# Score products of the mixers: the contraction over 128 partitions is replaced by one over the head's 64

## The chip, the cores and the metric

The program runs on one core of one Trainium2 chip. The metric is the device time of one execution in microseconds (us). The engines of the core are named as the profile names them: PE is TensorE's matmul, PEld its weight load, DVE is VectorE, ACT is ScalarE, POOL is GpSimd, SP is SyncE, which issues most of the transfers (DMA).

## The reference

Two blocks follow each other on 256 tokens of width 1024. The first has two layers; each is a SwiGLU, a token mixer and a second SwiGLU, every one with a modulation in front and a gated residual and layer norm behind. The second block has an attention and pooling mixer, a short convolution mixer and, after each, an expert-choice layer of 16 experts. The change touches the token mixer of the first block alone. It has three kinds of heads, four heads of each, and every one begins with products of queries and keys over a head width of 64:

```
# retention, chunks c of 128 tokens
scores = einsum('bhncd,bhnmd->bhncm', qc, kc) * decay_in
# dilated attention (causal windows)
sc = einsum('bhqd,bhqpjd->bhqpj', q_blk, k_g)       # softmax over the windows
# stick breaking
z = einsum('bhqd,bhsd->bhqs', q_blk, kf)            # log_sigmoid, reverse cumsum, exp
# out
y = concatenate([y_ret, y_dil, y_sb], -1) @ w_out
```

All of it is float32.

## The kernel before

Each engine has its own program, written out by hand, and they meet at semaphores. Weights stream from HBM into 12 slots of a tile `W`, with a second stream into `W_mod` for the modulation rows; SP issues both in a fixed order and waits before each transfer until the engines have freed its slot.

The mixer of a layer, on PE, is one straight list. `project(g, t, bank)` multiplies the tokens by 512 columns of w_in (line 768, 8 matmuls of 512 columns). `heads_turned` (line 781) transposes queries and keys of two heads, a pair, so that the 64 components of head 0 lie on partitions 0 to 63 and those of head 1 on 64 to 127. DVE or ACT copies the keys of the pair as they are into `kT` (a part of the tile that the trace calls `scr`) and the queries into `qm`, which has one slice of 128 partitions for each head: only the head's own 64 partitions are written, the other 64 were set to zero at the start. So a product over all 128 partitions gives the scores of that head alone.

There are six pairs b = 0 to 5 in a layer, in this order: dilated, stick, dilated, stick, retention, retention. For each, `scores(b)` makes the products for both heads into two PSUM banks (4 and 5 for even b, 6 and 7 for odd b): for each head one matmul with 128 moving columns and one with 256, either order. DVE then works on the pair (`maxima`, line 1656; `neg_abs`, line 1686; `decayed`, line 1720), ACT takes exponentials, `second(b)` on PE transposes the weights (line 805) or sums the sticks (lines 810 and 811), and `values(b)` multiplies by the values (lines 831 to 833). PE's order around these is: scores(0), project, scores(1), second(0), project, values(0), scores(2), second(1), project, values(1), scores(3), second(2), project, values(2), two times heads_turned, `row_sum` (line 659, 32 output columns in four column groups of the array), second(3), scores(4), values(3), scores(5), values(4), values(5), project, the transposes of the result (line 672) and the product by w_out (line 747).

`values(3)` waits for DVE's `stick_mask(3)` (lines 1692 and 1693), which stands on DVE behind `sticks(3)` (line 1705) and `decayed(4)` (line 1720). `second(1)` waits for DVE's `keeps(1)` (ends on line 1693).

A float32 matmul of the program is two passes in the trace: two weight loads and two MATMUL records.

Of the kernel before, what the change touches and what calls it, by code (L numbers as in the profile page):

```python
# [22 lines left out]
P = 128  # L23
S = 256
# [10 lines left out]
NH = 4  # L35
# [11 lines left out]
RET, DIL, STB = 0, 1, 2  # L47
# [95 lines left out]
def build(nc, A, out):  # L143
    with ExitStack() as ctx:
# [55 lines left out]
        qm = sb("qm", [P, 12, S])  # L200
        psum = ctx.enter_context(nc.psum_tensor("psum", [P, 8, 512], F32))
# [30 lines left out]
        kT = carve(6144, 6, S)  # L232
# [400 lines left out]
        def _(pe):  # L633
# [121 lines left out]
            def mixer(l):  # L755
# [28 lines left out]

                def scores(b):
                    kind, hb = ATT[b]
                    for hh in range(2):
                        q, k_ = qm[:, NH * kind + 2 * hb + hh, :], kT[:, 2 * kind + hb, :]
                        bk = psum[:, 4 + 2 * (b % 2) + hh, :]
                        if kind == DIL:  # L790
                            pe.matmul(bk[:, 0:P], q[:, 0:P], k_[:, 0:P], start=True, stop=True)
                            ins = pe.matmul(bk[:, P:3 * P], q[:, P:S], k_[:, :], start=True, stop=True)
                        else:
                            pe.matmul(bk[:, 0:S], k_[:, 0:P], q[:, :], start=True, stop=True)
                            ins = pe.matmul(bk[:, S:3 * P], k_[:, P:S], q[:, P:S], start=True, stop=True)
                    ins.then_inc(m_pe.sig(f"A{b}"), 1)

                def second(b):
# [104 lines left out]
            for job in range(FIRST_JOBS):  # L903
                pe.wait_ge(mod_taken, job + 1)
                for h in range(2):
                    ins = pe.matmul(psum[:, 2, 8 * job + h:8 * job + 8:2], first_row[job][:, P * h:P * h + P], ident[:, 0:97:32],
                                    start=True, stop=True)
# [19 lines left out]
            for t in range(TT):  # L927
# [4 lines left out]
                for kc in range(KC):  # L932
                    ins = pe.matmul(psum[:, t, 0:256], ctx_uT[:, kc, P * t:P * t + P], part(W[:, s, :], 0, KC, 256)[:, kc, :],
                                    start=(kc == 0), stop=(kc == KC - 1))
                ins.then_inc(m2_pe.sig(f"c{t}"), 1)
            turned(9)
            for t in range(TT):
                for b in range(3):
                    if t == 0 and b < 2:
                        pe.wait_ge(m2_act.s, m2_act.at(f"c{b}"))  # L940
                    for g in (2 * b, 2 * b + 1)[:1 if b == 2 else 2]:
                        s = in_slot("in", MIXIN_S[g]) if t == 0 else MIXIN_S[g]
                        for kc in range(KC):
                            ins = pe.matmul(psum[:, 3 * t + b, 256 * (g % 2):256 * (g % 2) + 256], uT[:, kc, P * t:P * t + P],  # L944
                                            part(W[:, s, :], 0, KC, 256)[:, kc, :], start=(kc == 0), stop=(kc == KC - 1))
# [3 lines left out]
            for i in range(2):  # L949
                for g in (2 * i, 2 * i + 1):  # L950
                    for t in range(TT):
                        ins = pe.matmul(psum[:, 2 + i, S * (g % 2):S * (g % 2) + S], proj2[:, t, 768 + P * g:768 + P * g + P],
                                        pool_c[:, g, t, :], start=(t == 0), stop=(t == TT - 1))
                ins.then_inc(m2_pe.sig(f"pool{i}"), 1)
            for i in range(2):
                pe.wait_ge(m2_dve.s, m2_dve.at(f"pool{i}"))
                for g in (2 * i, 2 * i + 1):
                    ins = pe.matmul(psum[:, 2 + i, S * (g % 2):S * (g % 2) + S], w_grp[:, g, :], pooledT[:, g, :],
                                    start=True, stop=True)
                ins.then_inc(m2_pe.sig(f"grp{i}"), 1)  # L960
            pe.wait_ge(m2_dve.s, m2_dve.at("rope"))
            for n, src in enumerate((ctx_kv[:, 0, 0:P], ctx_kv[:, 1, 0:P], proj2[:, 0, 512:640], proj2[:, 1, 512:640])):
                ins = pe.transpose(psum[:, 4, P * n:P * n + P], src, ident[:, :])
            ins.then_inc(m2_pe.sig("kT"), 1)
            for j in range(4):
                for t in range(TT):
                    c = S * (j % 2) + P * t
                    ins = pe.transpose(psum[:, 5 + j // 2, c:c + P], proj2[:, t, P * j:P * j + P], ident[:, :])
# [17 lines left out]
            for n in range(16):  # L986
# [5 lines left out]
                for c, v in enumerate((ctx_kv[:, 0, kv:kv + HD], ctx_kv[:, 1, kv:kv + HD],  # L992
                                       proj2[:, 0, 512 + kv:512 + kv + HD], proj2[:, 1, 512 + kv:512 + kv + HD])):
                    ins = pe.matmul(psum[:, t, HD * h:HD * h + HD], probT[:, n % 2, P * c:P * c + P], v,
                                    start=(c == 0), stop=(c == 3))
# [4 lines left out]
            for b in range(2):  # L1000
                for q in range(2):
                    for t in range(TT):
                        c = P * (2 * b + q)
                        ins = pe.transpose(psum[:, 4 + b, S * q + P * t:S * q + P * t + P], proj2[:, t, c:c + P], ident[:, :])
# [89 lines left out]
            for fb in range(KC):  # L1094
                if fb >= 2:
                    pe.wait_ge(cv_dve.s, cv_dve.at(f"f{fb - 2}"))
                for n in range(3):
# [3 lines left out]
                    o = psum[:, 4 + 2 * (fb % 2) + n // 2, S * (n % 2):S * (n % 2) + S]  # L1101
                    for kc in range(KC):
                        ins = pe.matmul(o, part(W[:, s, :], 0, KC, 256)[:, kc, P * (fb % 2):P * (fb % 2) + P], uT[:, kc, :],  # L1103
                                        start=(kc == 0), stop=(kc == KC - 1))
# [923 lines left out]
```

## Time and profile before

| | |
|---|---|
| median of 3 runs | 2522.92 us (2522.48 to 2528.18) |
| profiled execution, its own time | 2525.63 us |
| its span, first to last instruction | 2523.8 us |
| granted TensorE clock, mean | 0.881 |
| PE busy | 2078.4 us, 82% |
| DVE busy | 1118.6 us, 44% |
| ACT busy | 528.9 us, 21% |
| first mixer of the first block, first projection to the end of the w_out product | about 250 to 407 us from the start |
| second one | about 837 to 995 us |

Busy times overlap between engines. A row of the timeline that joins several instructions gives the start of the first, and the time to the end of the last; each MATMUL record is longer than the distance to the next one, since they are pipelined, so the cost of a matmul in a stream is read from the distance between starts.

### The profile page before, as it was taken

What the parts mean: (1) busy time and instruction counts of PE and PEld (TensorE: products, weight loads), DVE (VectorE), ACT (ScalarE), POOL (GpSimd) and SP (SyncE); (2) the same over time, 40 slices, a digit from 0 to 9 for tenths busy, and PEclk for the clock granted to TensorE, in tenths of its full rate; (3) what the DMA queues carried; (4) which work ended last, traced back from release to release, by engine and by line L of the source; (5) the groups of instructions that cost most, each with busy time, mean ns of one, the idle gap of its engine ahead of it and who ended that gap; (6) DMA issues with size and microseconds to landing.
All of it is one profiled execution on the core that took longest, in us unless ns stands there. A gap on an engine that the chain in (4) does not pass through costs nothing.

```text
span 2523.8 us, 33380 instructions
## 1 busy us (share of the span) xinstructions
PE 2078.4 (82%) x12372; PEld 1309.9 (52%) x12372; DVE 1118.6 (44%) x1724; ACT 528.9 (21%) x860; POOL 65.2 (3%) x96
## 2 busy tenths in 40 slices
PE   6998988997999887999877777777769777666664
PEld 4997455997999354999754322222238431111111
DVE  3887667788887676877343200000022320000002
ACT  3333133333333132333241100000010110000000
POOL 1000000000000000001000000000000000000000
PEclk9998999998999898999987977777779888888887
DMA  9986855887687765887602999999993389999996
GB/s 343 328 304 226 292 209 202 307 305 252 232 315 261 258 244 185 298 307 259 234 34 83 402 410 410 409 410 410 410 357 152 133 322 410 409 410 410 410 410 255
DMA packets 289371, 758.03 MB, mean 300 GB/s; under 512 B 17616, under 2 KB 125424, under 8 KB 289184
## 3 DMA queue, kind: packets, MB, share of 16 engines
q1 hardware_dynamic: 282368, 737.34, 77.8%
q0 software_dynamic: 6688, 19.78, 2.4%
q8 instruction: 36, 0.59, 0.1%
q14 instruction: 23, 0.19, 0.0%
q10 hardware_dynamic: 256, 0.13, 0.0%
HBM read 756.01 MB, written 1.18 MB: 300 GB/s over the span
## 4 chain that ended last, share of the span: by engine, by line
PE 54%; DMA 21%; SPq 13%; DVE 6%; issue 3%; ACT 2%; DVEq 1%; ACTq 0%
PE psum L707 20%; DMA W<-in_w_exp_up 16%; SPq L503 12%; PE psum L719 9%; PE psum L747 5%; PE psum L768 4%; PE psum L1103 3%; DMA W_mod<-in_mod_w 3%; PE psum L1042 3%; DMA W<-in_w_exp_down 1%; PE psum L944 1%; PE psum L680 1%; SPq L507 1%; ACT uT L1149 1%; PE psum L1054 1%
## 5 line engine op out<-in xcount | busy, mean ns | idle before, releaser
L707 PE MATMUL psum<-parts 128*128 128x256 f32 x4224 | 526.9, 285 | 16.2 <-DVE parts L1556 9.0
L707 PEld LDWEIGHTS psum<-parts 128*128 128x128 f32 x4224 | 524.3, 194 | 23.8 <-issue 17.6
L1042 PE MATMUL psum<-W,scr 128*32 128x512 f32 x2048 | 323.7, 743 | 136.3 <-DMA W<-in_w_exp_up 122.9
L1432 DVE SCALAR_TENSOR_TENSOR mod_acc<-W_mod,cond,mod_acc 128x1024 f32<-128x1024 f32 x196 | 251.8, 1284 | 51.6 <-issue 28.2
L1939 DVE TENSOR_TENSOR scr<-scr,psum 128x256 f32<-128x256 f32 x32 | 13.5, 421 | 581.3 <-ACT scr L1382 581.3
L719 PE MATMUL psum<-parts 128*128 128x512 f32 x1056 | 257.8, 393 | 0.0
L1042 PEld LDWEIGHTS psum<-W,scr 128*32 128x32 f32 x2048 | 53.8, 118 | 379.8 <-DMA W<-in_w_exp_up 287.5
L1556 DVE TENSOR_TENSOR parts<-W,parts 128x1024 fp32r<-128x1024 f32 x176 | 207.0, 1219 | 56.1 <-ACT parts L1179 56.1
L1067 PE MATMUL psum<-W,scr 128*32 128x256 f32 x2048 | 165.8, 463 | 73.6 <-DMA W<-in_w_exp_down 58.5
L719 PEld LDWEIGHTS psum<-parts 128*128 128x128 f32 x1056 | 192.6, 188 | 45.3 <-DVE parts L1569 8.2
L1079 PE MATMUL psum<-scr 128*128 128x512 f32 x256 | 160.1, 782 | 31.7 <-DVE scr L1952 29.7
L1179 ACT ACTIVATE parts<-W 128x1024 fp32r<-128x1024 f32 x176 | 175.7, 1051 | 46.4 <-issue 46.4
L768 PE MATMUL psum<-W,uT 128*128 128x512 f32 x384 | 176.6, 617 | 3.3 <-DVE uT L1476 3.3
L1067 PEld LDWEIGHTS psum<-W,scr 128*32 128x32 f32 x2048 | 65.4, 129 | 168.3 <-DMA W<-in_w_exp_down 102.9
L1382 ACT ACTIVATE scr<-psum 128x256 f32<-128x256 f32 x32 | 12.3, 384 | 612.1 <-PE psum L1042 612.1
L1952 DVE COPY scr<-psum 32x256 f32<-32x256 f32 x64 | 27.3, 426 | 244.6 <-PE psum L1067 244.2
L1079 PEld LDWEIGHTS psum<-scr 128*128 128x128 f32 x256 | 63.3, 262 | 117.7 <-issue 70.3
L768 PEld LDWEIGHTS psum<-W,uT 128*128 128x128 f32 x384 | 75.0, 199 | 93.5 <-issue 93.4
L1198 ACT ACTIVATE att<-psum 128x256 f32<-128x256 f32 x88 | 33.8, 384 | 378.6 <-PE psum L707 378.6
L1569 DVE TENSOR_TENSOR parts<-W,parts 128x1024 fp32r<-128x1024 f32 x88 | 107.2, 1218 | 10.3 <-ACT parts L1191 10.3
L1191 ACT ACTIVATE parts<-W 128x1024 fp32r<-128x1024 f32 x88 | 92.9, 1056 | 43.7 <-PE psum L719 43.7
L747 PE MATMUL psum<-W,uT 128*128 128x512 f32 x192 | 86.6, 611 | 2.7 <-issue 1.9
(283 smaller groups left out, 1641.1 us busy)
## 6 DMA issues: line engine op xcount, KB each, us to landing
W<-in_w_exp_down SPq DMA_DIRECT2D x128, 1024.0 KB
W<-in_w_exp_gate SPq DMA_DIRECT2D x256, 512.0 KB, 14.8
W<-in_w_exp_up SPq DMA_DIRECT2D x256, 512.0 KB, 15.7
W_mod<-in_mod_w SPq DMA_DIRECT2D x123, 1024.0 KB, 5.2
W<-in_ffn_w_gate SPq DMA_DIRECT2D x44, 1024.0 KB, 9.6
W<-in_ffn_w_up SPq DMA_DIRECT2D x44, 1024.0 KB, 12.0
W<-in_ffn_w_down SPq DMA_DIRECT2D x44, 1024.0 KB, 9.2
W<-in_w_in SPq DMA_DIRECT2D x24, 1024.0 KB, 8.5
```

What stands on the lines that cost most here:

```text
L503: sp.dma_start(W[:, s, D * n:D * n + D], w[layer, ds(e, 1), P * s:P * s + P, :] .rearrange("a p n -> p (a n)")).then_inc(landed[s], 16)
L707: ins = pe.matmul(psum[:, 4 + t % 2, S * g:S * g + S], w[:, t % 2, g, kc, :], u[:, kc, :], start=(n == 0 and kc == 0), stop=(n == 2 and kc ...
L719: ins = pe.matmul(psum[:, 2 * tt + h, :], h_[:, t % 2, P * tt:P * tt + P], w[:, t % 2, 512 * h:512 * h + 512], start=(t == 0 and n == 0), ...
L747: ins = pe.matmul(psum[:, 2 * tt + h, :], src[:, kc, P * tt:P * tt + P], w[:, kc % 2, 512 * h:512 * h + 512], start=(kc == 0), stop=(kc == ...
L768: ins = pe.matmul(psum[:, bank, :], uT[:, kc, P * t:P * t + P], part(W[:, s, :], 0, 4, 512)[:, kc % 4, :], start=(kc == 0), stop=(kc == KC ...
L1042: ins = pe.matmul(psum[32 * q:32 * q + 32, 4, :].rearrange("p (g n) -> p g n", g=2), xe_now[:, kc, :], w[:, :, q, :], start=(kc == 0), sto ...
L1067: ins = pe.matmul(psum[32 * q:32 * q + 32, 6, 0:256], e_hT[:, c % 2, 32 * (c // 2):32 * (c // 2) + 32], part(W[:, s, :], 0, 2, D)[:, c % 2 ...
L1079: ins = pe.matmul(psum[:, 2 * tt + h, :], GT[:, P * tt:P * tt + P], R[:, 512 * h:512 * h + 512], start=first, stop=True, skip_group_check= ...
L1179: ins = act.activation(gu_hi[:, t % 2, g, :, :], part(W[:, b + g, :], 0, KC, STEP)[:, :, P * (t % 2):P * (t % 2) + P], copy)
L1432: ins = dve.scalar_tensor_tensor(acc[:, :], w, col, acc[:, :], mul, add)
L1556: ins = dve.tensor_tensor(gu_lo[:, t % 2, g, :, :], part(W[:, b + g, :], 0, KC, STEP)[:, :, P * (t % 2):P * (t % 2) + P], gu_hi[:, t % 2, ...
L1569: dve.tensor_tensor(d_lo[:, t % 2, :], part(W[:, b + 2, :], 0, 2, D)[:, t % 2, :], d_hi[:, t % 2, :].bitcast(F32), sub).then_inc(lo_d, 1)
```

## The change

`scores(b)` reads only the 64 partitions of the head, of `qm` and of `kT` alike, so the contraction is over 64 rows. The loops are turned round: where one head had both its matmuls before the other head, now the first matmul of head 0 is followed by the first of head 1, and then come the two second ones. Head 0 uses the upper 64 rows of the array, head 1 the lower 64. Shapes of the outputs, banks, signals and waits are the same, and the zeros in `qm` are still written.

```
-                    for hh in range(2):
-                        q, k_ = qm[:, NH * kind + 2 * hb + hh, :], kT[:, 2 * kind + hb, :]
-                        bk = psum[:, 4 + 2 * (b % 2) + hh, :]
-                        if kind == DIL:
-                            pe.matmul(bk[:, 0:P], q[:, 0:P], k_[:, 0:P], start=True, stop=True)
-                            ins = pe.matmul(bk[:, P:3 * P], q[:, P:S], k_[:, :], start=True, stop=True)
-                        else:
-                            pe.matmul(bk[:, 0:S], k_[:, 0:P], q[:, :], start=True, stop=True)
-                            ins = pe.matmul(bk[:, S:3 * P], k_[:, P:S], q[:, P:S], start=True, stop=True)
+                    for half in range(2):
+                        for hh in range(2):
+                            rows_ = slice(64 * hh, 64 * hh + 64)
+                            q, k_ = qm[rows_, NH * kind + 2 * hb + hh, :], kT[rows_, 2 * kind + hb, :]
+                            bk = psum[:, 4 + 2 * (b % 2) + hh, :]
+                            if kind == DIL:
+                                o, w, x = ((bk[:, 0:P], q[:, 0:P], k_[:, 0:P]), (bk[:, P:3 * P], q[:, P:S], k_[:, :]))[half]
+                            else:
+                                o, w, x = ((bk[:, 0:S], k_[:, 0:P], q[:, :]), (bk[:, S:3 * P], k_[:, P:S], q[:, P:S]))[half]
+                            ins = pe.matmul(o, w, x, start=True, stop=True)
                     ins.then_inc(m_pe.sig(f"A{b}"), 1)
```

On PE, scores(2) stands between the last product of values(0) (line 833, now 834) and second(1) (line 810, now 811). Before, the four matmuls of a dilated pair alternate between 128 and 256 columns, one head after the other:

```order
L833 MATMUL psum<-scr 128x64
L791 MATMUL psum<-scr,qm 128x128
L792 MATMUL psum<-scr,qm 128x256
L791 MATMUL psum<-scr,qm 128x128
L792 MATMUL psum<-scr,qm 128x256
L810 MATMUL psum<-scr,k_later 128x384 [waits mixer_dve]
```

In the changed kernel the same place on PE reads as follows; `x2` is one matmul for each head, and the sizes are those of the output.

```order
L834 MATMUL psum<-scr 128x64
L796 MATMUL psum<-scr,qm 128x128 x2
L796 MATMUL psum<-scr,qm 128x256 x2
L811 MATMUL psum<-scr,k_later 128x384 [waits mixer_dve]
L812 MATMUL psum<-scr,k_ones 128x128
```

The second matmul of head 0 and the first of head 1 have changed places; nothing has moved across scores(2).

The second place is scores(4) on PE, of a retention pair, between second(3) (line 811, now 812) and values(3), whose first matmul waits for DVE. Before:

```order
L811 MATMUL psum<-scr,k_ones 128x128
L794 MATMUL psum<-qm,scr 128x256 [waits mixer_dve,mixer_act]
L795 MATMUL psum<-qm,scr 128x128
L794 MATMUL psum<-qm,scr 128x256
L795 MATMUL psum<-qm,scr 128x128
L831 MATMUL psum<-scr,tmp 128x64 [waits mixer_dve]
```

The changed kernel has at the same place on PE:

```order
L812 MATMUL psum<-scr,k_ones 128x128
L796 MATMUL psum<-qm,scr 128x256 [waits mixer_dve,mixer_act]
L796 MATMUL psum<-qm,scr 128x256
L796 MATMUL psum<-qm,scr 128x128 x2
L832 MATMUL psum<-scr,tmp 128x64 [waits mixer_dve]
```

Here too only the order within the group is another; the wait ahead of the group and the one behind it stand where they stood.

## Rows read from the trace of the kernel before

**Rows 1.** The page, busy time of the engines and shares of the chain
```profile
PE 2078.4 (82%) x12372; PEld 1309.9 (52%) x12372; DVE 1118.6 (44%) x1724; ACT 528.9 (21%) x860; POOL 65.2 (3%) x96
PE psum L707 20%; DMA W<-in_w_exp_up 16%; SPq L503 12%; PE psum L719 9%; PE psum L747 5%; PE psum L768 4%; PE psum L1103 3%; DMA W_mod<-in_mod_w 3%; PE psum L1042 3%; DMA W<-in_w_exp_down 1%; PE psum L944 1%; PE psum L680 1%; SPq L507 1%; ACT uT L1149 1%; PE psum L1054 1%
```

**Rows 2.** Groups of PE by line and form, the score products of both layers
```profile
L794 PE MATMUL psum<-qm,scr 128*128 128x256 f32 x32 | 9.8, 387 | 0.0
L795 PE MATMUL psum<-qm,scr 128*128 128x128 f32 x32 | 6.1, 274 | 0.0
L792 PE MATMUL psum<-scr,qm 128*128 128x256 f32 x16 | 4.8, 380 | 0.0
L791 PE MATMUL psum<-scr,qm 128*128 128x128 f32 x16 | 3.2, 281 | 0.0
```

**Rows 3.** Stretches of the first mixer: busy time, clock, DMA share
```profile
core 0: us, PE busy (x) PEld busy (x) DVE busy (x) ACT busy (x) POOL busy (x), PEclk, DMA share, GB/s
319.00:370.00 51.00, 49.00 (x212) 30.01 (x209) 36.05 (x90) 17.67 (x25) 4.05 (x5) 0.97 0.72 258
319.00:322.00 3.00, 3.00 (x10) 1.50 (x8) 2.82 (x5) 1.38 (x2) 0.00 (x0) 0.60 0.77 286
```

**Rows 4.** Timeline of PE, first mixer: start, us, what, [idle before]
```profile
318.69 0.87 PE L805 MATMUL psum<-k_ident,att 128*128 128x128 f32 x6 [3.20 <-DVE att L1668]
...
329.25 0.44 PE L791 MATMUL psum<-scr,qm 128*128 128x128 f32 x2
...
330.61 0.81 PE L810 MATMUL psum<-scr,k_later 128*128 128x384 f32 x2
...
354.05 0.60 PE L794 MATMUL psum<-qm,scr 128*128 128x256 f32 x2
354.49 0.38 PE L795 MATMUL psum<-qm,scr 128*128 128x128 f32 x2
354.71 0.60 PE L794 MATMUL psum<-qm,scr 128*128 128x256 f32 x2
355.14 0.38 PE L795 MATMUL psum<-qm,scr 128*128 128x128 f32 x2
357.39 0.41 PE L831 MATMUL psum<-scr,tmp 128*128 128x64 f32 x2 [1.87 <-DVE tmp L1693]
```

**Rows 5.** Timeline of PE around a group in four column tiles (L659)
```profile
350.67 1.04 PE L781 MATMUL psum<-k_ident,scr 128*128 128x128 f32 x8
351.64 0.64 PE L659 MATMUL psum<-mod_acc,k_ones 128*32 128x256 f32 x8
352.21 0.91 PE L810 MATMUL psum<-scr,k_later 128*128 128x384 f32 x2
352.96 0.38 PE L811 MATMUL psum<-scr,k_ones 128*128 128x128 f32 x2
353.18 0.81 PE L810 MATMUL psum<-scr,k_later 128*128 128x384 f32 x2
353.83 0.38 PE L811 MATMUL psum<-scr,k_ones 128*128 128x128 f32 x2
```

**Rows 6.** Timeline of PEld: loads of column tiles, full loads, few rows
```profile
304.20 0.19 PEld L659 LDWEIGHTS psum<-mod_acc,k_ones 128*32 128x32 f32 x8 [2.22 <-DVE mod_acc L1432]
...
305.73 0.30 PEld L791 LDWEIGHTS psum<-scr,qm 128*128 128x128 f32 x2
...
1374.12 0.29 PEld L1023 LDWEIGHTS psum<-k_ident,W_mod 16*128 16x128 f32 x2 [6.75 <-DVE W_mod L1916]
```

**Rows 7.** Timeline of DVE, ahead of second(1) and of values(3)
```profile
327.41 0.42 DVE L1693 TENSOR_TENSOR scr<-scr,k_strict 128x256 f32<-128x256 f32 x1
...
355.56 0.69 DVE L1720 TENSOR_TENSOR att<-psum,k_decay 128x512 f32<-128x512 f32 x1 [0.36 <-PE psum L795]
```

**Rows 8.** Timeline of PE, two projections of 16 passes each
```profile
319.40 8.73 PE L768 MATMUL psum<-W,uT 128*128 128x512 f32 x16
...
332.35 7.03 PE L768 MATMUL psum<-W,uT 128*128 128x512 f32 x16
```

## The prediction, made before the changed kernel ran

> **What bounds the kernel now.** I read the page first: PE is busy 82% of the span, and the chain of waits is led by the two lines of the SwiGLUs' matmuls (L707 and L719, 29% together), then by the expert weights (DMA and SP's queue for them, 28% in the first two entries) [rows 1]. The lines of the score products do not appear among the chain's first fifteen. Then the groups by form: the score products are 96 records, 48 matmuls of two passes, and their durations add up to 23.9 us [rows 2]. That sum counts overlaps twice, since a record is longer than the distance to the next; the timeline gives the real price. In scores(4) the starts are 354.05, 354.49, 354.71 and 355.14 [rows 4]: two passes of 256 columns take 0.44 us, two of 128 take 0.22, one head 0.65, a group 1.31. Twelve groups are at most 12 x 1.36 = 16.3 us, 0.6% of the time. The stretches come next: from 319 to 370 us PE is busy for 49.00 of 51.00 us at a granted clock of 0.97 [rows 3], so in this part of a mixer PE is the bound, and what PE saves there is saved, as far as nothing else takes over.
>
> **Which groups count.** scores(0) and scores(1) lie ahead of a wait of 3.20 us for DVE's weighting (L1668) [rows 4]; the chain there runs through the DMA of the modulation weights and DVE. Whatever PE gains in these two only lengthens that wait: 0. scores(2) runs from 329.25 to 330.61, 1.36 us, and PE goes straight on with second(1), whose input DVE finished at 327.41 + 0.42 = 327.83 [rows 4, 7]; its gain counts in full. scores(3) and scores(5) are of the same kind, between values and the next work of PE, in each of the two layers. scores(4) is followed by a wait of 1.87 us [rows 4]: values(3) waits for stick_mask(3), which stands on DVE behind decayed(4). DVE had been idle for 0.36 us when scores(4) released it [rows 7]; ahead of that it was still adding sticks(3), which depends on second(3) and not on the scores. So at most 0.36 us of scores(4)'s gain counts. Of a loss in scores(4), all would count.
>
> If g is the gain in one group, a layer gains 3 g + min(g', 0.36), where g' is that of scores(4), and the kernel twice that. The second layer shows the same list with the same waits at the same places.
>
> **What one group costs afterwards.** No row shows two matmuls in the two halves of the array, so the price is built from its nearest relative, L659: four matmuls of 256 columns in four column tiles, eight passes. At 0.22 us a pass they would take 1.73 us one after the other; they start at 351.64 and L810 starts at 352.21, so they took 0.57 [rows 5]. Two passes of 0.22 are 0.43, so the four tiles ran at the same time, and 0.14 us is left for staggered starts and for getting out of the tiles. Getting in: the eight transposes ahead start at 350.67 and take 8 x 0.11 = 0.88 to stream, to 351.55; L659 starts at 351.64, 0.09 to 0.10 later. And the first full matmul behind has to load its weights in the open: L810 to L811 takes 352.96 - 352.21 = 0.75 there and 353.83 - 353.18 = 0.65 the second time [rows 5], another 0.10.
>
> The two halves of a score group then cost, if they run at once:
> - into the tiles 0.10
> - first weights in the open (128 columns, as behind L659) 0.10
> - stream of one head, the other beside it, 0.65
> - stagger and out 0.14
> - first weights of the next full matmul in the open 0.10
>
> Together 1.09 us, against 1.36 for scores(2), (3) and (5) and 1.31 for scores(4). So g = 0.27 and g' = 0.22, which is under the cap. A layer gains 3 x 0.27 + 0.22 = 1.03, the kernel 2.1 us.
>
> The Trainium skill (TensorEngine Tiling (Array Packing), Key Properties) says that changing the tiling mode drains TensorE. The trace agrees for column tiles, by the 0.10 in and the 0.14 out above, and this speaks against the change: each of the twelve groups here stands alone between full-array work, so it pays both ways.
>
> **The bounds of the unknown.** Three prices can be off. First, the switch may cost nothing between row halves and the full array: then a group takes 0.65, g = 0.71, g' is cut to 0.36, and the kernel gains 2 x (3 x 0.71 + 0.36) = 5.0 us. Second, the halves may not overlap at all: a group is then 1.31 + 0.10 + 0.10 + 0.14 + 0.10 = 1.75, a loss of 0.39 in three groups and 0.44 in scores(4), 2 x 1.61 = 3.2 us. Third, the weight loads may go one after another. In L659 eight loads of 32 columns are done within 0.19 us, each some 0.11 long, so loads of different column tiles overlap [rows 6]. Those of a full array with 128 columns are 0.30 for two, and a load of only 16 rows with 128 columns is 0.29 for two [rows 6], so fewer rows make a load no shorter. In the stream of scores(4) a pass of 128 columns takes 0.11, which such a load just keeps up with. If the eight loads of a group cannot overlap between the halves, they are 8 x 0.11 = 0.88, with the last stream of 0.11 or 0.22 behind and 0.10 + 0.14 + 0.10 around: 1.33 to 1.44, a gain between +0.03 and -0.13 a group, or 2 x 4 x (-0.05) = -0.4 us, which is a loss of 0.4.
>
> I take the first sum, 2.1 us, since L659 is the nearest row. The Trainium skill (TensorE: Matmul & The Clock Gate, Part 3, The mechanism) says that LDWEIGHTS overlaps with matmuls in flight only when the row group differs. The trace differs: full-array loads run beside full-array matmuls in every group above, or a pair of 128-column passes could not come every 0.22 us. By the rule each half would pay four open loads, 4 x 0.11 + 0.65 = 1.09 before the switch costs, and the gain would be nothing, as in the third case.
>
> **What the gain meets later.** A mixer that ends 1 us earlier hands that to the SwiGLU, whose chain is PE's [rows 1], and the expert stream, bound by DMA, is started by slots that PE frees, so it starts earlier too. Engines released earlier inside the mixer (ACT and DVE) have waits for PE in this stretch, so they follow. Nothing on SP is moved: no wait and no transfer changes its place.
>
> **The rivals.**
> 1. Loads in a row, or halves that share more than the rows show: about -0.4 to +0.4 us, say 2522.9. For it: fewer rows don't shorten a load. Against: column tiles overlap fully.
> 2. The change has no effect on the array: 64 rows are treated as a full one. Then a group keeps 1.31 to 1.36 and the time stays at 2522.9.
> 3. Free switch: 5.0 us less, 2517.9. Against it stand the prices at L659.
> 4. Slower: the halves exclude each other and the switches are paid: 2526.1. It decides as soon as a group takes longer than 1.36 us; to be slower by over 0.3% (7.6 us) a group would have to take 1.3 + 7.6/8 = 2.3 us, for which no row speaks.
> 5. The clock. Behind the wait of 3.20 us the clock fell to 0.60 in the next 3 us, and a projection of 16 passes took 8.73 instead of 7.03 us [rows 3, 8]: 1.7 us. If thinner score groups or a wait lengthened by 0.3 us make it fall once more in each layer, the gain of 2.1 turns into a loss of 1.3: 2524.2. Against it: the same stretch behind keeps 1.00 or nearly so with waits of 1.87 us in it.
>
> **How the numbers follow.** The sum is made on the profiled execution, 2525.63 us, which lies 2.7 us above the median of the runs shown; the difference of 2.1 us is taken from the median, 2522.92 - 2.1 = 2520.8, and I give 2521.0. Chances: my sum 0.45, rivals 1 and 2 together 0.28, the free switch 0.11, exclusion of the halves 0.08, the clock 0.08. A measurement of this kernel can tell about 0.3% (7.6 us) from no change. All five lie within that: faster 0.03, same 0.93, slower 0.04, the small ones for a change of the clock's phase far behind the mixers that none of the sums holds. The range reaches from the free switch to exclusion: 2517.3 to 2526.2.
>
> **What would show it.** In the profile after, the first record of scores(2) to the first of second(1) (L796 to L811) should be 1.09 us apart instead of 1.36; the records of the two heads should start within 0.02 us of each other; the load of second(1) should show about 0.10 in the open; the wait of 1.87 us ahead of values(3) should stay, and DVE's idle time of 0.36 ahead of decayed(4) should shrink to 0.14. Wrong would be: starts of the four matmuls one after another at 0.11 and 0.22 (rivals 2 and 4), or a distance of 0.65 (rival 3). If the median moved by more than 7.6 us, the cause would not be in these groups, or they would cost twice what L659 shows.

## The result, and the profile after

The changed kernel is slower: 2535.23 us median of 9 runs (2526.01 to 2538.25) against 2522.92 us of the kernel before (2519.23 to 2531.15, 9 runs); the ratio is 1.0038, 95% interval [1.0022, 1.0054]. (The ratios of this document are the recorded ones, taken over all the runs of both kernels; they are not the quotients of the two medians, which would be 1.0049 here.) In a second set of runs it was 1.0040 [1.0026, 1.0053]. The profiled execution took 2536.32 us, its span is 2534.5 us.

The page's first row does not show the loss: PE is busy for 28 us less [rows 1]. That comes from the end of the program, where nothing was changed: in the last 1130 us PE is busy for 789 us at a clock of 0.84, where it was 826 us at 0.80. In the stretch of the first mixer that is timed below it is busy for 84.5 us, 3.7 more than before. The groups by form show the 96 records of the score products [rows 2], now on 64 rows; those of the stick and retention pairs (`psum<-qm,scr`) have grown from 387 to 499 ns and from 274 to 307 on average. Longer records are a first hint, and so is the granted clock of 0.90 from 319 to 370 us, where it was 0.97 [rows 3]:

```profile
PE 2050.6 (81%) x12372; PEld 1296.5 (51%) x12372; DVE 1119.6 (44%) x1724; ACT 528.5 (21%) x860; POOL 64.9 (3%) x96
...
L796 PE MATMUL psum<-qm,scr 64*128 64x256 f32 x32 | 6.7, 499 | 0.0
L796 PE MATMUL psum<-qm,scr 64*128 64x128 f32 x32 | 3.6, 307 | 0.0
...
L796 PE MATMUL psum<-scr,qm 64*128 64x256 f32 x16 | 2.4, 377 | 0.0
L796 PE MATMUL psum<-scr,qm 64*128 64x128 f32 x16 | 2.0, 322 | 0.0
...
319.00:370.00 51.00, 48.84 (x208) 30.50 (x209) 35.27 (x89) 17.57 (x24) 4.06 (x5) 0.90 0.72 258
```

The fall behind second(0) costs what it did: the projection there takes 8.73 us again [rows 8].

The score groups themselves did what was forecast, and a little more. The timeline of PE, first mixer (start, us, what, idle before), has these rows; line 796 is now the only line of the score products:

```profile
319.20 0.87 PE L806 MATMUL psum<-k_ident,att 128*128 128x128 f32 x6 [3.90 <-DVE att L1669]
...
329.86 0.93 PE L796 MATMUL psum<-scr,qm 64*128 64x128 f32 x8
330.71 0.91 PE L811 MATMUL psum<-scr,k_later 128*128 128x384 f32 x2
331.46 0.38 PE L812 MATMUL psum<-scr,k_ones 128*128 128x128 f32 x2
331.68 0.81 PE L811 MATMUL psum<-scr,k_later 128*128 128x384 f32 x2
332.33 0.38 PE L812 MATMUL psum<-scr,k_ones 128*128 128x128 f32 x2
...
353.99 0.92 PE L796 MATMUL psum<-qm,scr 64*128 64x256 f32 x8
356.87 0.41 PE L832 MATMUL psum<-scr,tmp 128*128 128x64 f32 x2 [1.96 <-DVE tmp L1694]
...
358.89 1.65 PE L796 MATMUL psum<-qm,scr 64*128 64x256 f32 x8
360.47 0.79 PE L832 MATMUL psum<-scr,att 128*128 128x128 f32 x2
```

From the first record of scores(2) to second(1) it is 0.85 us. Another 0.10 lies ahead of it, for getting into the tiles (from second(0) to scores(2) it is 10.66 us, where it was 10.56), and 0.10 behind it, where L811 to L812 takes 0.75 the first time and 0.65 the second. Together that is 1.05 us against 1.36 before [rows 4]. The records of line 796 from 329.5 to 331 us (duration in ns min/median/max, first and last start in us):

```profile
L796 PEld LDWEIGHTS psum<-scr,qm x8: 182/187/188, 329.9 to 330.2; 64*128 64x128 f32 x8
L796 PE MATMUL psum<-scr,qm x8: 272/374/378, 329.9 to 330.4; 64*128 64x128 f32 x4, 64*128 64x256 f32 x4
```

All eight loads are issued within 0.3 us, each 0.19 long, so the loads of the two halves overlap, and so do the passes. The records of the two heads start some 0.01 us apart, and within one half a load starts every 0.11 us, beside that half's own matmul. From second(0) to values(3) it is 356.87 - 319.20 = 37.67 us, where before it was 357.39 - 318.69 = 38.70 [rows 4]: 1.03 us gained in three groups, scores(2) to scores(4).

Then comes what was not forecast. scores(5) takes 1.65 us, from 358.89, though it is the same work as scores(4) with 0.92. The stretches of the changed kernel show why. Columns: us, busy time and instructions of PE, PEld, DVE, ACT, POOL, then the granted clock, DMA share and GB/s:

```profile
354.00:357.50 3.50, 1.54 (x15) 1.34 (x14) 2.63 (x5) 2.13 (x2) 0.00 (x0) 1.00 1.03 420
357.60:361.00 3.40, 3.40 (x18) 2.89 (x17) 0.41 (x1) 0.00 (x0) 0.00 (x0) 0.51 1.02 408
361.00:364.40 3.40, 3.40 (x18) 3.40 (x17) 0.95 (x3) 0.00 (x0) 0.00 (x0) 0.50 1.09 350
...
374.70:384.80 10.10, 7.37 (x21) 4.93 (x22) 6.29 (x9) 6.91 (x10) 0.00 (x0) 0.50 0.07 13
384.90:394.00 9.10, 9.10 (x22) 4.07 (x22) 6.01 (x6) 0.00 (x0) 0.00 (x0) 1.00 0.58 216
```

The same places in the kernel before:

```profile
357.60:361.00 3.40, 3.40 (x28) 3.30 (x28) 0.68 (x2) 0.00 (x0) 0.00 (x0) 1.00 1.03 412
361.00:364.40 3.40, 3.40 (x22) 2.60 (x21) 2.04 (x10) 0.00 (x0) 0.00 (x0) 1.00 1.07 351
...
374.20:377.60 3.40, 3.37 (x16) 3.28 (x16) 0.51 (x2) 2.02 (x5) 0.00 (x0) 0.50 0.00 0
377.70:394.00 16.30, 15.41 (x43) 6.64 (x43) 12.88 (x14) 4.26 (x5) 0.00 (x0) 1.00 0.36 130
```

A granted clock of 0.50 is the lower of TensorE's two levels, 1.2 GHz, and 1.00 is 2.4 GHz. In the kernel before, the clock stays up after the wait ahead of values(3) and is down for 3.4 us at the transposes of the result, behind their wait of 4.36 us. In the changed kernel it is down for 6.8 us from 357.6, when PE has been running again for 0.7 us after its wait, and for 10.2 us from 374.7. The second mixer shows the same pair.

So the mixer is slower by more than it gained. From the start of second(0) to the start of the last matmul by w_out (L747), the profiled executions have 87.9 us in the first mixer and 87.8 in the second before, 91.7 and 91.6 after: 3.8 us a mixer, 7.6 in all. The groups themselves gained about 1.4 us a mixer (measured further down, with the clock at 2.4 GHz throughout), so the clock took 5.2 a mixer. The other 3.1 us between the two spans lie mostly behind the second mixer (1529.7 against 1533.0 us to the end), where nothing was changed; over all traces of this study that part varies from 1522.5 to 1533.0, so one execution says nothing about it. By the ratio the whole loss is 9.6 us; the two mixers show 7.6 of it, and the place of the rest is not shown.

### The profile page after: what moved, and what is told of

Read it like the earlier page. It is cut to its first block, busy times and chain, and to the rows that moved or that the text cites. A ratio compares the mean times of both kernels' runs of the same rounds, so it can differ in the third digit from the quotient of the medians.

```text
span 2534.5 us, 33380 instructions
## 1 busy us (share of the span) xinstructions
PE 2050.6 (81%) x12372; PEld 1296.5 (51%) x12372; DVE 1119.6 (44%) x1724; ACT 528.5 (21%) x860; POOL 64.9 (3%) x96
## 4 chain that ended last, share of the span: by engine, by line
PE 54%; DMA 21%; SPq 12%; DVE 6%; issue 3%; ACT 2%; DVEq 1%; ACTq 0%
PE psum L707 20%; DMA W<-in_w_exp_up 16%; SPq L503 11%; PE psum L719 9%; PE psum L747 5%; PE psum L768 4%; PE psum L1104 3%; PE psum L1043 3%; DMA W_mod<-in_mod_w 3%; SPq L507 1%; DMA W<-in_w_exp_down 1%; PE psum L945 1%; PE psum L680 1%; ACT uT L1150 1%; PE psum L1055 1%
## 5 line engine op out<-in xcount | busy, mean ns | idle before, releaser
L1043 PEld LDWEIGHTS psum<-W,scr 128*32 128x32 f32 x2048 | 53.0, 120 | 400.6 <-DMA W<-in_w_exp_up 316.0
L1068 PE MATMUL psum<-W,scr 128*32 128x256 f32 x2048 | 157.4, 437 | 97.2 <-DMA W<-in_w_exp_down 82.1
L1080 PE MATMUL psum<-scr 128*128 128x512 f32 x256 | 140.8, 700 | 31.7 <-DVE scr L1953 29.6
L1068 PEld LDWEIGHTS psum<-W,scr 128*32 128x32 f32 x2048 | 60.5, 120 | 185.9 <-DMA W<-in_w_exp_down 130.3
L1199 ACT ACTIVATE att<-psum 128x256 f32<-128x256 f32 x88 | 33.7, 383 | 377.7 <-PE psum L707 377.7
L1080 PEld LDWEIGHTS psum<-scr 128*128 128x128 f32 x256 | 55.4, 229 | 106.6 <-issue 58.9
L747 PE MATMUL psum<-W,uT 128*128 128x512 f32 x192 | 90.4, 633 | 2.6 <-issue 1.8
```

The lines of the kernel that those rows point to most:

```text
L747: ins = pe.matmul(psum[:, 2 * tt + h, :], src[:, kc, P * tt:P * tt + P], w[:, kc % 2, 512 * h:512 * h + 512], start=(kc == 0), stop=(kc == ...
L1043: ins = pe.matmul(psum[32 * q:32 * q + 32, 4, :].rearrange("p (g n) -> p g n", g=2), xe_now[:, kc, :], w[:, :, q, :], start=(kc == 0), sto ...
L1068: ins = pe.matmul(psum[32 * q:32 * q + 32, 6, 0:256], e_hT[:, c % 2, 32 * (c // 2):32 * (c // 2) + 32], part(W[:, s, :], 0, 2, D)[:, c % 2 ...
L1080: ins = pe.matmul(psum[:, 2 * tt + h, :], GT[:, P * tt:P * tt + P], R[:, 512 * h:512 * h + 512], start=first, stop=True, skip_group_check= ...
```

## The experiments

Eighteen kernels ran. Two theories were held against each other. Theory D (for delay): the clock falls at a wait or not by the moment at which the wait comes, and the change moved the wait ahead of values(3) by 1.03 us. Theory A: groups of 64 rows do less for the clock. Ratios are to the kernel before, with 95% intervals; medians are of 12 runs where nothing else is said. Five kernels (f2, h1, i1, i2, k2) leave out a part of the work, as is said at each. Between runs a kernel spreads over some 14 us (the one before: 2518.45 to 2532.37 in 35 runs), so the ratio is what counts.

**The order of the loops alone.** In the changed `scores`, `qm[rows_, ...]` and `kT[rows_, ...]` are `qm[:, ...]` and `kT[:, ...]` again.

> The turned loops alone: the four matmuls of a group alternate between the heads, but contract over all 128 partitions as before. Theory A (the extra time of the changed kernel, 9.6 us by the ratio, is TensorE's clock falling once more in each mixer, behind scores(4), because the 64-row groups do less or leave PE idle longer) expects the time of the kernel before within 0.3% (2523), groups of 1.31 to 1.36 us and a granted clock of 1.00 from 356 to 372 us. Rival B (the order of banks or heads costs something later) expects part or all of the 9.6 us here.

Measured: 2525.0 us, ratio 0.9996 [0.9986, 1.0007]. Rival B falls. But its trace has a clock of 0.79 from 354 to 370 us in the first mixer, and 1.00 in the same place of the second:

```profile
354.00:370.00 16.00, 14.13 (x73) 11.67 (x66) 7.21 (x21) 4.05 (x5) 0.00 (x0) 0.79 1.06 391
941.00:957.00 16.00, 14.13 (x96) 11.21 (x95) 9.42 (x23) 5.03 (x7) 0.00 (x0) 1.00 0.99 373
```

(0.79 over 16 us is 6.8 us at half rate, 0.89 is 3.4 us.) So the clock can fall there with full rows too. The kernel before may do it in some executions, which would explain part of its spread; its one trace does not show it. Theory A alone can't stand.

The same trace shows that the place after second(0) is not the whole of the moment. In both mixers the wait ends 38.7 us after second(0), but the clock's fall behind second(0) does not come at the same place:

```profile
322.30:325.60 3.30, 3.30 (x5) 1.35 (x4) 3.06 (x7) 2.83 (x3) 0.00 (x0) 0.50 1.00 400
325.70:359.50 33.80, 31.96 (x141) 19.67 (x139) 25.12 (x54) 14.41 (x21) 4.06 (x5) 1.00 0.57 206
912.80:916.10 3.30, 3.30 (x8) 1.75 (x7) 3.06 (x7) 1.83 (x2) 0.00 (x0) 0.50 0.92 304
916.20:951.00 34.80, 32.96 (x143) 20.06 (x142) 26.06 (x55) 15.40 (x22) 4.06 (x5) 1.00 0.59 211
```

values(3) starts at 359.53 and 951.04 us. From the clock's return to that it is 33.9 us in the mixer where the clock falls again and 34.9 in the one where it does not.

**Part of the pairs.** `rows_` is the head's 64 for the pairs named and all 128 for the others, in the old order.

> 64-row products in scores(2) and scores(3) only, the other four pairs as before. Theory A expects the clock to stay at 1.00 from 356 to 372 us, since the place of the fall (scores(4), the wait ahead of values(3), scores(5)) is as before, and a small gain: 2 layers x 2 groups x 0.32 us = 1.3 us, so 2521.6. Rival C (any 64-row group brings a fall, or the falls come from a shift of the program's time against the clock) expects 4 to 9 us more than before.

Measured: 2526.5 us, 1.0005 [0.9990, 1.0020]; clock 0.89 in the first mixer and 1.00 in the second, with the wait at 38.0 us. No gain is seen (the 1.3 us expected lie inside the interval), and no clear loss.

> 64-row products in scores(4) and scores(5) only. Theory A expects the whole loss here: the clock at half rate for some 7 us around scores(5) and values(4), and longer at half rate behind the wait at the transposes of the result, together 4.4 us a layer, so 2532. Rival C expects no more than in the run with scores(2) and scores(3).

Measured: 2526.35 us, 1.0009 [0.9994, 1.0025]; clock 1.00 in the first mixer, 0.79 in the second. The wait is at 38.2 and 38.3 us. I had put the whole loss here; that was wrong. Neither half of the change brings it alone.

**The old order with 64 rows.** The two loops of the changed `scores` are exchanged.

> 64-row products everywhere, but in the old order: both matmuls of head 0, then both of head 1. If the two halves only overlap when their matmuls alternate, a group keeps about 1.3 us plus some 0.4 for the switches, PE is not idle for longer, and theory A in the form that idle time counts expects no fall and 2 x 4 x 0.4 = 3 us more than before (2526); in the form that half-filled rows count it expects the fall and 2533 to 2536. If the halves overlap in this order too, the group takes 0.85 us and all is as in the changed kernel.

Measured: 2533.45 us, 1.0029 [1.0015, 1.0043]. In its timeline a group takes as long as in the changed kernel:

```profile
329.92 0.93 PE L796 MATMUL psum<-scr,qm 64*128 64x128 f32 x8
330.78 0.91 PE L811 MATMUL psum<-scr,k_later 128*128 128x384 f32 x2
```

A group takes 0.86 us here and 0.85 in the changed kernel, so the two halves run at the same time whichever order the matmuls have. Its trace has stretches of 3.4 us in the first mixer, and of 6.8 and 10.2 in the second.

**Moving the wait.** A delay in the changed kernel (f1), and a shortening in the one before (f2, which leaves out the last eighth of the contraction of project(1,1)):

```
# f1_delay, ahead of project(1, 1, 1), in the changed kernel
for _ in range(2): pe.matmul(psum[:, 1, 0:S], ident[:, :], K["windows"][:, :], start=True, stop=True)
pe.matmul(psum[:, 1, 0:P], ident[:, :], K["windows"][:, 0:P], start=True, stop=True)
# f2_short, in project, in the kernel before
n = KC - 1 if (g, t) == (1, 1) else KC      # for kc in range(n)
```

> The changed kernel, with 1.07 us of full-array matmuls of constants (two of 256 columns, one of 128) put ahead of project(1,1), into the bank that this projection then overwrites. All six groups keep their 64 rows, the wait ahead of values(3) keeps its length, but comes 38.7 us after the start of second(0) again, as in the kernel before, where the changed kernel has 37.7. Theory D (the clock falls in that wait or not by the moment at which it comes; the change moved it by 1.03 us into the bad moment) expects no fall at values(3) in most executions and about the time of the kernel before: 2.06 gained, 2.15 added, so 2525, within 0.15%. Theory A (64-row groups do too little for the clock) expects the changed kernel's time plus 2 us: 2535 to 2537.

Measured: 2524.67 us, 0.9995 [0.9978, 1.0012]. All groups have 64 rows, 1.07 us a layer of useless work was added, and the loss is gone. From second(0) to the last w_out matmul its second mixer takes 87.5 us; the first, where the clock fell at values(3) in this execution, 92.0. Its waits are those of the changed kernel, 1.96 us ahead of values(3), so the 0.1 us by which that wait is longer than before does not bring the loss by itself.

> The kernel before, full rows everywhere, but project(1,1) leaves out the last eighth of its contraction in both layers (two passes of 512 columns, 0.86 us a layer), so one block of the values is wrong. The wait ahead of values(3) then comes 0.86 us earlier after second(0). Theory D expects the falls of the changed kernel without any 64-row product: 1.7 us less work, some 9 to 11 us from the clock, so 2531 to 2534. Theory A expects 2525 - 1.7 = 2523.

Measured: 2527.26 us, 1.0012 [0.9997, 1.0027], with a clock of 0.89 at values(3) in both mixers and 10.2 us at half rate at the transposes in both. So a kernel with full rows, given 1.7 us less work, gets no faster and, by the middle of its interval, rather slower. But it is 3 us and not the 6 to 9 that theory D expected.

> The changed kernel with project(1,1) leaving out the last eighth of its contraction (0.86 us a layer), so that the wait ahead of values(3) comes 36.8 us after second(0) where the changed kernel has 37.7. Theory D expects that this goes past the bad moment: no fall at values(3) in most executions, so 2519 to 2526, 8 us or more less than the changed kernel for 1.7 us less work. Theory A, or any cause that goes with the amount of work, expects 2531 to 2534.

The kernel h1 is the changed one with the shortening of f2. Measured: 2526.61 us, 1.0009 [0.9995, 1.0023], 0.3% below the changed kernel for 1.7 us (0.07%) less work. Its trace has falls at values(3) all the same, of 3.4 us in both mixers, so "no fall" was wrong and the length of the stretch is what went down.

**Rows or place.** The same places, with full rows and with 64. In the kernel before, `i1_short103` and `i2_short189` leave out one and two eighths of project(1,1), and 96 of 512 columns of the one before (`m = 416 if n < KC and kc == n - 2 else 512`); `i3_delay02` is the changed kernel with one 128-column matmul of constants ahead of project(1,1).

> The kernel before, full rows, with project(1,1) leaving out the last eighth of its contraction and, of the eighth before, the last 96 columns: 1.03 us a layer less, so the wait ahead of values(3) comes 37.7 us after second(0), as in the changed kernel. Theory D alone (only the moment of the wait counts) expects the changed kernel's time: ratio 1.003 to 1.004, half-rate stretches of 7 us at values(3) and 10 us at the transposes. Theory D with A (64-row groups also do less for the clock) expects 1.000 to 1.002 and shorter stretches.

> The kernel before, full rows, with project(1,1) leaving out two eighths and 96 columns of a third: 1.89 us a layer less, the wait at 36.8 us as in the changed kernel shortened by 0.86 (ratio 1.0009, with stretches of 3.4 us at values(3)). Theory D alone expects the same ratio, 1.000 to 1.002. D with A expects less than that by more than 0.1%, and no fall at values(3).

> The changed kernel with one full-array matmul of 128 columns of constants (0.22 us) ahead of project(1,1): the wait at 37.9 us, where the full-row kernel with 0.86 us less had it (ratio 1.0012). Theory D alone expects about that ratio, 1.001 to 1.002, a steep drop from the changed kernel's 1.0038 for 0.2 us of delay. D with A expects 1.003 to 1.004.

> The changed kernel once more, for a second trace and for its time beside the three others: 1.002 to 1.005, and half-rate stretches at values(3) and, longer than before, at the transposes in both mixers.

Medians: 2525.73 us (i1), 2524.07 (i2), 2534.43 (i3), 2533.63 (i4, the changed kernel again). All ratios, by the place of the wait:

| second(0) to values(3) | full rows | 64 rows |
|---|---|---|
| 38.7 us | 1 (before) | 0.9995 [0.9978, 1.0012] (f1) |
| 37.9 us | 1.0012 [0.9997, 1.0027] (f2) | 1.0032 [1.0019, 1.0045] (i3) |
| 37.7 us | 1.0011 [1.0001, 1.0021] (i1) | 1.0040 [1.0026, 1.0053] (i4) |
| 36.8 us | 0.9993 [0.9981, 1.0004] (i2) | 1.0009 [0.9995, 1.0023] (h1) |

Both columns rise and come down again, while the full-row kernels only lose work: i1 does 2.1 us less than the kernel before, a ratio of 0.9992, and its interval lies above that. The place counts. And at 37.9 and 37.7 us the kernels with 64 rows are 0.20% and 0.29% above those with full rows; in the second of these pairs the intervals do not meet. So both theories hold a part. (i2 had been expected without a fall at values(3); its trace has 3.4 us there in both mixers.) The traces agree. Of i1, first mixer:

```profile
358.70:362.10 3.40, 3.40 (x14) 3.04 (x14) 0.00 (x0) 0.00 (x0) 0.00 (x0) 0.50 1.02 416
362.20:365.60 3.40, 3.40 (x27) 3.05 (x27) 1.88 (x6) 0.00 (x0) 0.00 (x0) 1.00 1.07 352
375.80:379.20 3.40, 2.94 (x14) 2.94 (x15) 0.49 (x2) 1.59 (x5) 0.00 (x0) 0.50 0.00 0
379.30:386.00 6.70, 5.70 (x16) 2.62 (x15) 5.75 (x8) 4.69 (x5) 0.00 (x0) 1.00 0.34 109
```

The clock is back at 1.00 after 3.4 us, where in the changed kernel it stays down for 6.8. Over the mixers with the wait at 37.7 to 37.9 us, those with 64 rows (the changed kernel twice, i3, e4) have a stretch of 6.8 us at values(3) in 7 of 8, those with full rows (f2, i1) have 3.4 us in three of 4 and none in one. (In one mixer of i4 a longer fall ahead had pushed the wait to 38.3 us.)

Mixers with the same place after second(0) differ, as in e1. By the time from the clock's return behind second(0) to values(3), the traces without fillings sort better:

| return to values(3) | stretch at values(3) |
|---|---|
| 32.3 to 33.0 us | 3.4 us in all 6 mixers, of 64 rows and of full rows |
| 33.2 to 33.5 us, scores(4) and (5) with full rows | 3.4 us in all 6 (e2, f2 twice, i1, k2 twice) |
| 33.2 to 33.5 us, with 64 rows | 6.8 us in all 5 (after twice, e4, i3, i4) |
| 33.7 to 34.2 us | 6.8 us in 6 of 7, e1 with full rows among them; none in one (i1) |
| 34.3 us and more | none in all 6, f1 with 64 rows among them |

So at the same moment the two kinds of group part cleanly between 33.2 and 33.5 us; elsewhere in these traces the moment decides, except perhaps at 34.1 us, where i1 with full rows has no fall beside e3 and f1 with 6.8 us. The sorting was found in the traces afterwards; no kernel was built to test it. The kernels with 64 rows in scores(4) also wait 1.96 us ahead of values(3) and not 1.87, which no run holds apart from the rows.

**Which group, and rows or time.** `k1_full5`: `rows_ = slice(0, P) if b == 5 else ...` in the changed kernel. `k2_onehead5`: i1 with `range(1 if b == 5 else 2)` over the heads, so that scores(5) leaves out its second head.

> The changed kernel with scores(5) alone back to 128 rows; scores(0) to scores(4) keep 64. The wait ahead of values(3) stays where the changed kernel has it. If the 64-row scores(5), which comes right behind the first half-rate stretch has begun, is what prolongs it, the stretch at values(3) is 3.4 us long instead of 6.8 and the ratio falls from 1.004 to 1.001 to 1.002. If the other groups or the place alone do it, the ratio stays at 1.003 to 1.004.

Measured: 2530.86 us, 1.0023 [1.0013, 1.0034]. The stretch at values(3) is 3.4 us in its first mixer and 6.8 in the second:

```profile
357.50:361.00 3.50, 3.50 (x15) 3.14 (x15) 0.14 (x1) 0.00 (x0) 0.00 (x0) 0.52 1.02 400
361.00:364.40 3.40, 3.40 (x27) 2.92 (x26) 1.98 (x7) 0.00 (x0) 0.00 (x0) 1.00 1.10 348
944.60:948.00 3.40, 3.40 (x15) 3.22 (x15) 0.00 (x0) 0.16 (x1) 0.00 (x0) 0.50 1.02 410
948.00:951.40 3.40, 3.40 (x15) 3.22 (x15) 1.35 (x3) 0.00 (x0) 0.00 (x0) 0.50 1.07 358
```

The ratio lies between those of full rows and of 64, just above the 1.001 to 1.002 expected, and its interval overlaps that of the changed kernel: by the ratio, scores(5) seems to be about half of what the rows cost, and that is not settled. The stretches do not help: these two mixers lie at 33.0 and 34.0 us from the clock's return, where e4 with 64 rows throughout has 3.4 us too, and e1 with full rows 6.8.

> Full rows everywhere, the wait ahead of values(3) at the changed kernel's place (1.03 us left out of project(1,1) as before), and scores(5) computes head 0 only, so it takes 0.65 us of PE in place of 1.31, about as long as the 64-row group; its second head is left out. If less PE time in this group prolongs the half-rate stretch, the ratio rises from 1.0011 to about 1.003 with stretches of 6.8 us; if it is the 64 rows as such, it stays at 1.0005 to 1.001 (0.65 us a layer less work) with stretches of 3.4 us.

Measured: 2522.85 us, 0.9991 [0.9978, 1.0003], below the 1.0005 to 1.001 expected, with stretches of 3.4 us in both mixers. Halving the time of scores(5) with full rows does no harm, so it is not PE's time in that group. Whether it is the 64 rows as such, the gaps on entering and leaving the tiles, or the wait that is 0.09 us longer was not told apart.

**Filling the waits.** Full-array matmuls of constants into a free PSUM bank, n of 256 columns:

```
def keep_busy(n, bank):
    for _ in range(n):
        pe.matmul(psum[:, bank, 0:S], ident[:, :], K["windows"][:, :], start=True, stop=True)
# behind scores(4):          keep_busy(3, 2)    f3, f4, h2, g1, g2
# behind project(2, 1, 4):   keep_busy(8, 7)    h2, g1, g2
# behind scores(1):          keep_busy(7, 2)    g1, g2
```

> The changed kernel, with three full-array matmuls of constants (1.3 us) into a free bank behind scores(4), inside the wait of 1.96 us ahead of values(3). Theory D expects that the wait left is too short for a fall at any moment: no fall at values(3), and the gain of the groups is seen at last: 2525 - 2.1 and less for the executions of the kernel before that fell there, so 2520 to 2523. If the falls are caused by something else than this idle time, it stays at 2533.

Measured: 2530.94 us, 1.0007 [0.9990, 1.0023]: not the 2520 to 2523 expected. (Its runs fall in two lots, five from 2520.65 to 2526.53 us and seven from 2530.72 to 2538.03, and the median lies in the upper lot.) In its trace the fall at values(3) is gone from both mixers, and one of 10.2 us is left at the transposes in both; the first mixer:

```profile
354.00:370.00 16.00, 15.05 (x78) 9.75 (x76) 9.32 (x34) 2.97 (x5) 0.00 (x0) 1.00 1.05 389
371.90:382.10 10.20, 7.32 (x21) 4.89 (x22) 6.24 (x9) 7.05 (x10) 0.00 (x0) 0.50 0.08 12
```

> The kernel before with the same three matmuls in the same wait. Theory D expects a small gain, since only some executions of the kernel before fall at values(3): 2521 to 2525, and 2 us more than the changed kernel with the same filling. Its lowest time should stay at that of the kernel before, 2518.5.

Measured: 2524.85 us, 0.9994 [0.9980, 1.0008]: as before within the interval, so not the 2 us above f3 that was expected. f3 still pays the long stretch at the transposes in both mixers, f4 in one of two (3.4 us in the other).

> The changed kernel with the fillings ahead of values(3) and ahead of the transposes of the result, not the one ahead of second(0). With the one ahead of values(3) alone the ratio was 1.0007 and the profile had half-rate stretches of 10 us at the transposes. Theory D expects both to be gone: 2516 to 2520. If it is not below 2525, the stretch at the transposes is not caused by the wait ahead of them.

Measured (10 runs): 2519.53 us, 0.9979 [0.9968, 0.9990], as expected, with no half-rate time at either place in its trace.

> The changed kernel with full-array matmuls of constants in all three long waits of a mixer: 7 (3.0 us) behind scores(1), ahead of second(0); 3 (1.3 us) behind scores(4), ahead of values(3); 8 (3.4 us) behind project(2,1), ahead of the transposes of the result. Theory D expects no half-rate stretch between the first projection and the w_out product: 2.1 us of the groups, 2 x 1.7 for the stretch behind second(0) and 2 x 2 to 2 x 4 for the one at the transposes, so 2512 to 2517, and less spread. If idle time were not what lets the clock fall, it would stay near the run with one filling (2526 to 2531).

> The kernel before with the same three fillings. Theory D expects 2514 to 2519: with the clock taken out of the comparison the changed groups are worth their 2.1 us, so this one should lie 1.5 to 2.5 us above the changed kernel with the fillings. If the two are equal, or this one is faster, the 64-row groups have no gain of their own.

Measured: g1 (5 runs) 2514.34 us, 0.9959 [0.9946, 0.9972]; g2 (7 runs) 2518.33 us, 0.9976 [0.9962, 0.9990]. Both beat both kernels, and the changed one with fillings has the lowest ratio of the study, some 10 us below the kernel before. Its timeline around the wait ahead of values(3), and its stretch over the second mixer:

```profile
353.73 0.92 PE L796 MATMUL psum<-qm,scr 64*128 64x256 f32 x8
354.58 1.56 PE L839 MATMUL psum<-k_windows,k_ident 128*128 128x256 f32 x6
356.61 0.41 PE L832 MATMUL psum<-scr,tmp 128*128 128x64 f32 x2 [0.46 <-DVE tmp L1701]
...
358.06 0.92 PE L796 MATMUL psum<-qm,scr 64*128 64x256 f32 x8
```
```profile
840.00:990.00 150.00, 143.80 (x515) 74.48 (x513) 102.86 (x178) 36.71 (x56) 4.62 (x6) 1.00 0.63 225
```

scores(5) takes 0.92 us again, and the clock is 1.00 throughout. From second(0) to the last w_out matmul the mixers take 83.4 us in g1 and 84.8 in g2, in both layers: with the clock out of the way the change is worth 1.4 us a mixer, 2.8 in all. The runs agree but don't settle it: the two ratios are 0.17% apart, 4.3 us, and their intervals overlap.

## Why the prediction was wrong, point by point

- **What bounds the mixer there: right.** PE does, and g1 shows the gain once the clock stays up. Which groups count was right too: in the changed kernel the wait ahead of second(0) grew from 3.20 to 3.90 us, which swallowed the gain of scores(0) and scores(1).
- **The price of a group: right in mechanism, 0.04 us off in size.** 1.05 us measured for 1.09, built from the column tiles of L659. Getting in costs 0.10, the open load behind 0.10. (The sign given, 1.09 us from scores(2) to second(1), was put wrongly: those two 0.10 lie outside that distance, which is 0.85.) The cap of 0.36 on scores(4) was reached: DVE's row for decayed(4) has no idle time left, where it had 0.36 before [rows 7], against the 0.14 forecast.

```profile
354.10 0.95 DVE L1706 TENSOR_TENSOR tmp<-tmp,psum 128x768 f32<-128x768 f32 x1 [0.74 <-PE psum L812]
354.97 0.68 DVE L1721 TENSOR_TENSOR att<-psum,k_decay 128x512 f32<-128x512 f32 x1
```

- **The sum of 2.1 us: an underestimate.** 2.8 us, measured between the traces of g1 and g2. The groups as measured give 0.5 of the 0.7 us between: 0.04 in three of them and 0.14 in scores(4), twice.
- **Loads in a row (rival 1): wrong.** The loads of the halves overlap, and so do those within one half. The Trainium skill (TensorE: Matmul & The Clock Gate, Part 3, The mechanism) lets a load overlap with matmuls in flight only where the row group differs; the trace disagrees, since by it a group would take the 1.09 us before the switches that the prediction worked out, and the group takes 1.05 with them.
- **"What the gain meets later": this is the step that failed.** It said that a mixer that ends 1 us earlier hands that on, and put nothing for the clock inside the mixer. The mixer ended 3.8 us later instead, because the waits inside it came at other moments and the clock was at half rate behind two of them. Place alone cost a full-row kernel some 5 us: i1 is at 1.0011 in spite of 2.1 us less work.
- **The clock (rival 5): the right mechanism, mis-sized, with too small a chance.** It was priced at one fall of 1.7 us a layer, and its counter-argument was that the same stretch kept 1.00 with a wait of 1.87 us in it. One trace showed that for one moment of the wait; the trace of the order experiment shows full-row groups with a fall there. Measured: two stretches, 6.8 us where there was none and 10.2 us where there were 3.4, about 5.2 us a mixer. The part that comes with the 64 rows, 0.29% or 7 us at the same place, was not thought of beyond the words "thinner score groups".
- **The stated range ended at 2526.2** because its ends were two prices of the groups, a free switch and exclusion of the halves. Rival 5's 2524.2 lay inside it; a clock that takes 5.2 us a mixer was nowhere in it.

## What to carry to other kernels

Where PE waits for some microseconds in a stage, a change that saves one microsecond ahead of the wait can cost five, as here, because it moves the wait and the clock falls; ask of each wait of PE in the stretch what a fall there would cost, and count it as a real case. To judge a small PE change, compare it with the waits filled, or at several delays, and not by one placing. Filling the waits with matmuls that nothing reads took 0.24% off the kernel before and 0.41% off with this change, more than the change itself could give (0.11%, 2.8 us).

## What the runs showed of the hardware

- Two 64-row tiles of the array, with float32 matmuls of two passes, run at the same time, with their weight loads: 0.85 us from the first record to the next full-array matmul for what takes 1.31 to 1.36 with 128 rows, or 1.05 with the getting in and out. It doesn't matter whether the matmuls alternate between the tiles (0.86 in e4).
- The moment of a clock change is not that of an event on PE. In the changed kernel the fall came 0.8 us after PE had started again in the first mixer and 0.7 in the second; in the kernel before, the same wait, which comes 1.0 us later after second(0), was followed by none; in e1 it was followed by one in the first mixer and by none in the second. The Trainium skill (TensorE: Matmul & The Clock Gate, Part 1) describes the window over which the gate watches TensorE as free-running, so that it does not start over with the kernel. The traces agree with that as far as they go: in e1's two mixers the same wait stands 33.9 and 34.9 us behind the clock's last change.
- With 64-row groups around it, the stretch at half rate behind a wait lasted 6.8 us in 7 of 8 mixers, with full rows at the same place 3.4 in three of 4; at 33.2 to 33.5 us from the clock's last return it is 6.8 us in 5 of 5 against 3.4 in 6 of 6. Why is open: the rows, the gaps at the tiles and a wait of 1.96 us in place of 1.87 were not held apart.
